# A four-part MLP whose down products also run in 1024-column groups with seven-product pairs

## What is computed

```python
h  = h + (g_mla * y_mla + g_fox * y_fox) @ w_out        # end of the attention half
hn = rmsnorm(h, mlp_norm)
u  = square(relu(hn @ w_up))                            # (256, 2048) @ (2048, 8192)
h  = h + u @ w_down                                     # (256, 8192) @ (8192, 2048)
out = rmsnorm(h, final_norm)
```

## Time and profile before

| what | us |
|---|---|
| median of 3 runs | 1275.11 |
| the profiled execution | 1275.99 |
| its span, first to last instruction | 1274.2 |
| PE busy | 1260.2 (5618 matmuls) |
| DVE busy | 851.7 |
| ACT busy | 640.9 |
| mean granted TensorE clock | 0.999 |

### The profile page before, as it was taken

One profiled execution on the slowest core, in us unless ns is written; L12 is line 12 of the kernel. 1 busy time (PEld: TensorE's weight loads), 2 busy tenths in 40 slices (PEclk: granted clock), 3 DMA queues, 4 the chain that ended last, 5 costly groups with the idle time before them and its releaser, 6 DMA issues.

```text
span 1274.2 us, 14512 instructions
## 1 busy us (share of the span) xinstructions
PE 1260.2 (99%) x5618; PEld 1044.1 (82%) x5618; DVE 851.7 (67%) x897; ACT 640.9 (50%) x748; POOL 137.6 (11%) x239
## 2 busy tenths in 40 slices
PE   9999999999999999999999999999999999999997
PEld 7888888888888888887888878888788887788886
DVE  6676566646776677678889875454568988654544
ACT  6654345445555444455655654333355655553443
POOL 0022001103221111110111110000001101100000
PEclk9999999999999999999999999999999999999999
DMA  8798856755886688776777786566557677866563
GB/s 324 257 305 264 264 177 208 226 196 191 267 274 213 198 301 276 226 254 198 245 246 262 236 276 209 193 197 193 189 182 246 221 257 244 289 195 215 196 194 120
DMA packets 83141, 293.90 MB, mean 231 GB/s; under 512 B 11320, under 2 KB 12416, under 8 KB 82432
## 3 DMA queue, kind: packets, MB, share of 16 engines
q1 hardware_dynamic: 67536, 243.04, 57.8%
q0 software_dynamic: 14528, 48.00, 12.1%
q10 hardware_dynamic: 1008, 1.92, 0.4%
HBM read 269.45 MB, written 23.47 MB: 230 GB/s over the span
## 4 chain that ended last, share of the span: by engine, by line
PE 85%; DVE 7%; DMA 4%; ACT 2%; issue 1%; POOL 0%; DVEq 0%; ACTq 0%; POOLq 0%
PE bank L655 67%; PE bank L701 6%; PE bank L702 6%; PE bank L703 5%; DMA raw<-weights 3%; DVE hl L1210 3%; ACT hl L961 1%; DVE wsum_lo L1227 1%; DMA kn<-turn_rows 1%; DVE wsum L1220 1%; PE bank L842 1%; ACT hid L1027 0%; DVE blocks L1407 0%; PE bank L824 0%; PE bank L822 0%
## 5 line engine op out<-in xcount | busy, mean ns | idle before, releaser
L1210 DVE TENSOR_TENSOR hl<-raw,hl 128x1024 fp32r<-128x1024 f32 x451 | 547.5, 1230 | 345.2 <-ACT hl L961 344.2
L961 ACT ACTIVATE hl<-raw 128x1024 fp32r<-128x1024 f32 x451 | 470.4, 1056 | 460.4 <-PE bank L655 369.6
L655 PE MATMUL bank<-hl,u_hl 128*128 128x512 f32 x1536 | 348.8, 389 | 1.6 <-DVE hid L1266 1.6
L655 PE MATMUL bank<-hl,x_hl 128*128 128x512 f32 (+1 forms) x1536 | 344.9, 385 | 0.0
L655 PEld LDWEIGHTS bank<-hl,u_hl 128*128 128x128 f32 x1536 | 288.1, 188 | 62.3 <-DVE hid L1266 2.4
L655 PEld LDWEIGHTS bank<-hl,x_hl 128*128 128x128 f32 x1536 | 284.0, 188 | 56.9 <-DVE hl L1201 0.6
L701 PE MATMUL bank<-hl,hn_hl 128*128 128x512 f32 x432 | 168.6, 390 | 3.1 <-DVE resid L1483 1.6
L703 PE MATMUL bank<-hl,hn_hl 128*128 128x512 f32 x432 | 168.1, 389 | 0.0
L702 PE MATMUL bank<-hl,hn_hl 128*128 128x512 f32 x432 | 168.1, 389 | 0.0
L701 PEld LDWEIGHTS bank<-hl,hn_hl 128*128 128x128 f32 x432 | 81.1, 188 | 21.8 <-issue 3.8
L703 PEld LDWEIGHTS bank<-hl,hn_hl 128*128 128x128 f32 x432 | 81.1, 188 | 17.0
(11 more groups left out here) (189 smaller groups left out, 787.0 us busy)
## 6 DMA issues: line engine op xcount, KB each, us to landing
raw<-weights SPq DMA_DIRECT2D x454, 512.0 KB, 4.4
turn_rows<-blocks POOLq DMA_DIRECT2D x34, 512.0 KB, 4.3
turned<-turn_rows POOLq DMA_DIRECT2D x96, 128.0 KB, 3.5
prob_rows<-prob_blocks POOLq DMA_DIRECT2D x8, 384.0 KB, 2.8
prob_t<-prob_rows POOLq DMA_DIRECT2D x32, 96.0 KB, 5.5
turned_h<-turn_rows POOLq DMA_DIRECT2D x20, 128.0 KB, 5.0
x_rows<-x_n POOLq DMA_DIRECT2D x2, 1024.0 KB, 7.8
resid<-x_n POOLq DMA_DIRECT2D x1, 2048.0 KB, 10.9
```

Of the source, the lines that this page charges most:

```text
L655: return nc.tensor.matmul(bank[:, gr.pair + tb, 0:gr.cols], tile[:, k, x_part, tb * P:tb * P + P], w, start=k == 0 and not x_part and not ...
L961: nc.scalar.activation(hl[:, slot, 0], raw[:, slot], ACT.Copy).then_inc(unit_hi, 1)
L1210: nc.vector.tensor_tensor(hl[:, slot, 1], raw[:, slot], hl[:, slot, 0].bitcast(F32), ALU.subtract).then_inc(unit_split, 1)
```

## The change

The MLP is cut into four parts of 2048 hidden columns, each with two up groups and two down passes' groups of 1024 columns over 16 tiles. Of the last part only the first 1024 columns are such a group; the last 1024 columns stay two groups of 512. Every 1024-column group, down ones too, has the pairs (4,5) and (10,11) in seven products. For that:

- DVE makes the row sums of u (`u_sums`) at the hand-off, and the weight sums are now made earlier: the first (`two_sums`) right after lo of the unit two before the pair, the others (`other_sums`) one unit later.
- From the ninth unit of up0 on there are eight raw slots (four more in `raw_more`). The first use of the new ones waits for w_out's end. The ring `hl` keeps four.
- The norm's factor is applied by ReLU (two ACT instructions with a scale in place of one), so its square root is taken in up0's first group, and down results are added unscaled.
- A down group's results go straight into the residual: `into_resid` (after the seven products) and `totals_into_resid` (banks 0 to 3).

```diff
-MLP_PARTS = 2
+DEEP_RING = 8
+MLP_PARTS = 4
@@ make_groups
-        for g in range(CHUNKS):
-            add(f"down{part}", g, K_FF)
+        for g in range(CHUNKS // 2 if part < MLP_PARTS - 1 else 1):
+            add(f"down{part}", g, K_FF, 0, 1, 2 * WIDE)
+    for g in range(CHUNKS // 2, CHUNKS):
+        add(LAST_DOWN, g, K_FF, 2 * (g % 2))
@@ make_due
+        if gr.double:
+            due[gr.u0 + 14].append(("p1 copied", gr))
+            due[gr.u0 + 14].append(("products summed", gr))
+            due[gr.last + 2].append(("totals", gr))
...
+                if piece.g in IN_CHUNK:
+                    due[gr.last + 10 + 4 * c].append(("u summed", piece))
+            if gr.n == 0:
+                due[gr.u0 + 6].append(("mlp mean", gr))
+                due[gr.u0 + 8].append(("mlp root", gr))
@@ SP
-                sp.wait_ge(unit_split, u - RING + 1)
-                sp.dma_start(raw[:, slot_of(u)], stream[u]).then_inc(unit_loaded[slot_of(u)], 16)
-                if u == BY["down1", 0].u0 + RING:
-                    sp.wait_ge(unit_used, BY["down1", 0].u0)
+                if RAW_BEFORE[u] is None:
+                    sp.wait_ge(unit_used, BY["w_out", CHUNKS - 1].last + 1)
+                else:
+                    sp.wait_ge(unit_split, RAW_BEFORE[u] + 1)
+                sp.dma_start(raw_unit(u), stream[u]).then_inc(unit_loaded[RAW_SLOT[u]], 16)
+                if u == BY[LAST_DOWN, 0].u0 + RING:
+                    sp.wait_ge(unit_used, BY[LAST_DOWN, 0].u0)
                     sp.dma_start(gain_rows[:], final_gain.partition_broadcast(P)).then_inc(gain_rows_in, 16)
@@ DVE
+            def two_sums(u):
+                n, b = SEVEN_AT[u], u + 1
+                dve.wait_ge(unit_loaded[RAW_SLOT[u]], RAW_NTH[u] * 16)
+                dve.wait_ge(unit_loaded[RAW_SLOT[b]], RAW_NTH[b] * 16)
+                if n:
+                    dve.wait_ge(seven_summed, n)
+                nc.vector.tensor_tensor(wsum[:, 0:2], raw_unit(u)[:, WIDE:].unsqueeze(1).broadcast_to([P, 2, WIDE]),
+                                        raw_units(u, 2)[:, :, 0:WIDE], ALU.add).then_inc(wsum_pair, 1)
...
+            def into_resid(gr):
+                left, right = chunk(2 * gr.g), chunk(2 * gr.g + 1)
+                dve.wait_ge(p1_copied, gr.n + 1)
+                dve.wait_ge(totals_done, gr.freed[0] - 1)
+                nc.vector.tensor_tensor(resid[:, 0, left], resid[:, 0, left], bank[:, 4], ALU.add)
+                then_wait(nc.vector.tensor_tensor(hid[:, 0], bank[:, 6], hid[:, 1], ALU.subtract))
+                then_wait(nc.vector.tensor_tensor(hid[:, 2], hid[:, 0], bank[:, 7], ALU.add))
+                nc.vector.tensor_tensor(resid[:, 1, left], resid[:, 1, left], hid[:, 2], ALU.subtract)
+                nc.vector.tensor_tensor(hid[:, 3:5], hid[:, 0:3:2], bank[:, 5].unsqueeze(1).broadcast_to([P, 2, WIDE]),
+                                        ALU.add).then_inc(products_summed, 1)
+                dve.wait_ge(products_summed, gr.n + 1)
+                then_wait(nc.vector.tensor_tensor(resid[:, :, right], resid[:, :, right], hid[:, 3:5], ALU.add))
...
             for u in range(N_UNITS):
                 if u in SEVEN_AT:
-                    weight_sums(u)
+                    two_or_third_to_lo(SEVEN_AT[u], 1, slice(2, 3))
                 unit_to_lo(u)
                 after(u)
+                if u + 2 in SEVEN_AT:
+                    two_sums(u + 2)
+                if u + 1 in SEVEN_AT:
+                    other_sums(u + 1)
                 for what, g in DUE[u]:
@@ ACT, hidden_squares
-                z = hid[:, 1 + 2 * c:3 + 2 * c]
-                nc.scalar.activation(z, z, ACT.Relu).then_inc(positive, 1)
+                act.wait_ge(rstd_col_done, MLP_NORM + 1)
+                for tb in range(TB):
+                    ins = nc.scalar.activation(hid[:, 1 + 2 * c + tb], hid[:, 1 + 2 * c + tb], ACT.Relu,
+                                               scale=rstd_col[:, MLP_NORM, tb:tb + 1])
```

More of the change, by code:

```diff
@@ L78, with pairs_by_seven @@
 SEVEN = (4, 10)
-SUMS = {k: n for n, k in enumerate(SEVEN)}
 IN_CHUNK = {k // 4: n for n, k in enumerate(SEVEN)}
+def pairs_by_seven(name, g):
+    return SEVEN
+LAST_DOWN = f"down{MLP_PARTS - 1}"
 def make_groups():
@@ L160, in number_groups @@
             had[2] = gr
+            gr.seven = pairs_by_seven(gr.name, gr.g)
+            gr.seven0, n_seven = n_seven, n_seven + len(gr.seven)
+            if gr.name[:2] == "up":
+                gr.m, n_up = n_up, n_up + 1
+                gr.freed = [n_totals + i for i in (1, 2, 3, 4)]
+            else:
+                gr.freed = [n_totals + i for i in (1, 1, 2, 3)]
+            n_totals = gr.freed[-1]
         elif gr.name == "gates":
@@ L167, with raw_slots @@
 number_groups()
+DOUBLES = [gr for gr in GROUPS if gr.double]
+DEEP_FROM = BY["up0", 0].u0 + DEEP_RING
+def raw_slots():
+    slot, nth, before, had = [], [], [], {}
+    for u in range(N_UNITS):
+        s = u % (DEEP_RING if u >= DEEP_FROM else RING)
+        earlier = had.setdefault(s, [])
+        before.append(earlier[-1] if earlier else None)
+        earlier.append(u)
+        slot.append(s)
+        nth.append(len(earlier))
+    return slot, nth, before
+RAW_SLOT, RAW_NTH, RAW_BEFORE = raw_slots()
+assert DEEP_FROM % DEEP_RING == 0
 TURNED = [("cq", 0), ("keys", 0), ("fq", 0), ("fq", 1), ("fk", 0), ("fk", 1),
@@ L200, in make_due @@
             after(middle, "mixed", 4 + gr.g)
+        if gr.double:
+            due[gr.u0 + 14].append(("p1 copied", gr))
+            due[gr.u0 + 14].append(("products summed", gr))
+            due[gr.last + 2].append(("totals", gr))
+        if gr.double and gr.name == LAST_DOWN:
+            for c in range(2):
+                due[gr.last + 3 + c].append(("chunk squared", Chunk(gr.name, 2 * gr.g + c)))
         if gr.name[:2] == "up":
-            due[gr.u0 + SEVEN[-1] + 4].append(("p1 copied", gr))
-            due[gr.u0 + SEVEN[-1] + 4].append(("products summed", gr))
-            due[gr.last + 2].append(("totals", gr))
             for c in range(2):
@@ L222, in make_due @@
             continue
-        later = {("fq", 0): 5, ("fq", 1): 4, ("ukv_k", 0): 2, ("w_out", CHUNKS - 1): -1,
-                 ("down0", CHUNKS - 1): -1}.get((gr.name, gr.g), 0)
+        later = {("fq", 0): 5, ("fq", 1): 4, ("ukv_k", 0): 2, ("w_out", CHUNKS - 1): -1}.get((gr.name, gr.g), 0)
         after(gr.last + later - (gr.units == 1), "group", gr)
@@ L241, in make_due @@
     for work in due:
-        work.sort(key=lambda it: not (it[0] == "group" and it[1].name in ("w_out", "down0")))
+        work.sort(key=lambda it: not (it[0] == "group" and it[1].name == "w_out"))
     return due
@@ L376, in program @@
         bank = ctx.enter_context(nc.psum_tensor("bank", [P, 8, 512], F32))
-        unit_loaded = [sem(f"unit_loaded{i}") for i in range(RING)]
+        unit_loaded = [sem(f"unit_loaded{i}") for i in range(DEEP_RING)]
         unit_hi = sem("unit_hi")
@@ L486, in slot_of, with raw_units, raw_unit, sums_before @@
             return u % RING
+        def raw_units(u, count):
+            s = RAW_SLOT[u]
+            return raw[:, s:s + count] if s < RING else raw_more[:, s - RING:s - RING + count]
+        def raw_unit(u):
+            return raw_units(u, 1)[:, 0]
+        ROW_SUMS = {"w": (sums, sums_hl), "u": (u_sums, u_sums_hl)}
+        def sums_before(name):
+            return 0 if name == "w_out" else len(SEVEN) * (int(name[2:]) + 1)
+        def sums_of(name):
+            return {"up": sums_hl, "do": u_sums_hl}[name[:2]]
         def chunk(g):
@@ L639, in wait_for_banks @@
                     return
[L640 to L641 removed]
+                if had.double:
+                    pe.wait_ge(totals_done, had.freed[gr.pair + 1])
                 elif had.name in ("keys", "fq") and gr.name[0] == "u":
@@ L754, in double_group @@
                 k = 0
-                if gr.before.name[:2] != "up":
+                if not gr.before.double:
                     for c in range(2):
@@ L1608, in pack_stream @@
             stream[gr.unit[k // gr.slabs], :, at:at + gr.cols] = w[k]
-        if gr.cols == 2 * WIDE:
-            for k in SEVEN:
+        if gr.double:
+            for k in gr.seven:
                 stream[gr.unit[k + 1]] = np.concatenate([w[k + 1][:, WIDE:], w[k + 1][:, :WIDE]], axis=1)
```

209 lines of the change are left out of this document (125 added, 84 removed).

## The result

The changed kernel takes 1289.6 us (median of 4 runs, 1288.4 to 1291.6) against 1274.9 for the kernel before: ratio 1.0114, 95% interval 1.0095 to 1.0134, so 1% slower. The forecast was 1284, the range 1275 to 1293. Its profiled execution has a span of 1287.9, 13.7 more than before.

A forecast was written before the change was run, and what follows sets the result against it. PE, busy 1260.2 of 1274.2 us, was taken as the bound. Span 1274.2 - 13.5 + 12.0 + 3.3 + 7.0 = 1283.0, plus 1.8 outside it 1284.8, so 1284 for a median; range 1275 to 1293.

The forecast's parts named there:

- the likeliest case: Whole kernel: the forecast's own case, a time of 1279 to 1288 us, chance 0.50.
- 42 matmuls, waits of before that go: Seven down groups save 42 matmuls (9.5 us); waits at up1, down passes and a weight sum go: gain 13.5.
- lo(15), six down groups: Six DVE instructions before lo(15) make PE wait: 1.8 us in three groups, 2.2 in three, 12.0 together.
- down3's first group: PE loses 1.4 us at lo(3), 3.8 at the chunk for unit 8, 1.9 at lo(15); taken as 7.0.
- the chain over 28.3: First groups of down passes: second chunk's rounding at 28.3 us delays lo(15) until 39.3; PE waits 2.2.
- Row sums of u fall into DVE's idle time: Up groups: four short instructions and a low part cost nothing; lo(15) then ends just at 37.4.
- The seam: Start of up0: the weight sum ahead of w_out's addition waits for a load; PE waits 3.3 us more.
- The clock's fall: Rival at up0's start: 4.7 us idle halves the clock, at most 2.4 more, 1286 us; chance 0.10.
- gain_rows: Down3's first group: this load holds back units 5 and up; lo(3) and the first chunk come late, 7.0 with lo(15).
- Late hand-offs in the other passes: Rival: first chunk takes 16.8 us in the other three passes too, 6.6 more, 1290 us; chance 0.14.
- DVE in time: Rival: DVE and ACT run far enough ahead that lo(15) brings no waits, 1270 us; chance 0.12.
- half of it: Rival: each wait at lo(15) is 1.0 us and gain_rows costs 3.6, 1275 us, no change; chance 0.14.

The follow-up runs named there:

- experiment 3: Changed kernel with the down groups' sums of the seven products one unit later, behind lo(15) instead of ahead of it: 1281.4 us, ratio 1.0049.
- experiment 8: Kernel before the change, with the last of the sums of the seven products of its eight up groups done three times over: 1296.0 us, ratio 1.0165.
- experiment 9: Changed kernel with plain products in the down groups (no weight sums, no row sums of u, no sums of three banks): 1285.0 us, ratio 1.0068.
- Experiments 2: Changed kernel with the load of the gain rows in down3's first group five units later on SP's queue: 1281.7 us, ratio 1.0056.
- experiment 7: Changed kernel with four slots of raw weights instead of eight: 1324.2 us, ratio 1.0376.
- experiment 4: Changed kernel with up0's first weight sums behind w_out's last addition, gain rows' load five units later, down groups' sums one unit later: 1270.5 us, ratio 0.9966.
- experiment 5: Kernel of experiment 4 with the sums of the seven products one unit later in the eight up groups too: 1270.5 us, ratio 0.9967.

## Why the prediction was right, and where its steps were not

It had the sign and most of the mechanisms, and the time fell in its range. It fell 1.6 above 1288, the upper end of the likeliest case. That the sum came as near as it did is in part luck: the terms below that were too small are short by 9.7 in all, those that were too large are over by 4.8.

| step | forecast | measured in the trace after |
|---|---|---|
| 42 matmuls, waits of before that go | -13.5 | -9.5 and -5.8 |
| lo(15), six down groups | +12.0 | 6 x 1.5 = +9.0 |
| lo(15) in up groups | 0 | +2.9 |
| start of up0, wait | +3.3 | +3.4 |
| start of up0, clock | 0 (a rival) | +1.5 |
| down3's first group | +7.0 | 1.7 + 6.3 + 2.2 + 1.5 = +11.7 |
| other, from 300 us on | 0 | +0.5 |

The right column adds to 13.7, the difference of the spans.

- **lo(15)** is shown from both sides: experiment 3 takes the waits away, experiment 8 makes such waits in the other kernel. The size was 1.5 and not 1.8 to 2.2; groups that follow an up group are no worse than the others, so the extra 0.3 for the second chunk (the chain over 28.3) was wrong.
- **"Row sums of u fall into DVE's idle time"** is the step that failed with no term of its own. The step called the up groups' lo(15) just in time, without a margin, and yet put 1.7 us of new work shortly ahead of it at nothing. The traces showed 1.5 and 1.4 lost there. The second half of the cause is the landing of the second chunk, which varies from kernel to kernel (0 to 1.4 lost in up1) and makes up0's wait in experiment 9 without any row sums; the prediction followed that chunk only into the down groups.
- **The seam** was right to 0.1. The clock's fall was called a rival at 0.10; it came true and cost 1.5, where my bound was 2.4. The Trainium skill, "TensorE: Matmul & The Clock Gate", section "Why this matters for your kernels", advises against idle gaps in mid-kernel because the clock drops; the trace agrees for this gap of 4.78, and the rule deserved more than 0.10.
- **gain_rows** was mis-sized. The lateness of lo(3) was 1.7 for 1.4, but for the hand-off I took the 16.8 of a kernel with four slots. With eight, the held queue sent seven loads in some 9.5 us, the hand-off took 19.6, PE lost 6.3 at it in place of 3.8, and the idle time then brought the clock down (2.2). Experiments 2, 7 and 9 show the burst as the cause of the added time. The prediction also gave `gain_rows` as what made the 16.8 longer than the 14.4 of up0's end; but POOL's pause of 2.6, which stands at this place in every kernel, is by itself as large as that difference.
- **Late hand-offs in the other passes** (rival, 0.14) did not occur in the changed kernel: the one wait on L1565 is down3's.
- **DVE in time, and half of it**, are out by the waits of 1.5 and by experiment 8.

## What to carry to other kernels

On an engine that works in order, an edit's price is its length less the slack of the next instruction that the bound engine waits for; with hardly any slack nearly all of it is paid in each group (2.1 of 2.5 us in experiment 8), and moving it behind that instruction gave 8.3 of 10.5 us back. A load that is held in a queue holds all behind it: with a deeper ring of slots more of them go at once when it is released, and here they slowed the transfers on which the bound engine waits (a 512 KB store from 3.6 to 6.1 and 8.0). The saving of 42 matmuls became a gain only when three such places had been put right, each with an edit of one or a few lines (0.3%; 0.6% with two moves more).

## What was not expected of the hardware

The clock fell after shorter idle times than I had thought. PE's waits behind which it fell lasted 2.00, 2.02 and 2.74 in experiment 8 and 2.77 in experiment 4, 2.17 in experiment 5, 2.20 and 2.42 in experiment 7, and all of 3.8 to 7.5 in six kernels; it stayed up behind others of 1.99, 2.02, 2.19 and 2.37 in experiment 8 and behind all of 1.4 to 1.9. Behind the waits of 2.0 to 2.8 it fell only when PE was at work again, 0.1 to 1.4 us after its first matmul; the same holds for six of the longer ones (3.8 to 4.6). In experiment 4 PE resumed at 1198.59 and the starts were 0.24 apart at first, then 0.43 from 1200.20 to 1203.19, 1.5 us lost. A wait of 2.8 us cost as much by the clock as one of 4.8.

POOL's pause of 2.59 us before one load of down3's first chunk was not expected either. It stands in all eleven kernels and was part of the 16.8 from which I reckoned.
